# A packed row table read and written by indirect DMAs, weight rings of six slots split in place, and the next expert's rows turned after the last turn

## What is computed

```python
logits = xf @ w_router + b_router
top_logit, top_idx = lax.top_k(logits, 2)
top_w = softmax(top_logit)
# each position is a row of two experts; for the rows of expert e:
out = (silu(xb @ w1[e]) * (xb @ w3[e])) @ w2[e]
# y[position] = sum over its two experts of top_w * out
```

## Time and profile before

| | |
|---|---|
| median of 3 runs | 1771.09 us (1769.48 to 1774.81) |
| the profiled execution | 1762.26 us, its span 1760.5 us |
| mean granted clock of TensorE in it | 0.98 |
| TensorE busy (matmuls) | 1648.9 us, 94% |
| VectorE busy | 1357.8 us, 77% |
| ScalarE busy | 1022.7 us, 58% |
| GpSimd busy | 69.7 us, 4% |
| read from HBM, written to it | 518.85 MB, 15.47 MB |

### The profile page before, as it was taken

The page is one execution under the profiler, slowest core; times in us unless marked ns, Lnnn a source line. Parts: engine busy times, 40 slices in busy tenths (PEclk is TensorE's granted clock), DMA queues, the critical chain, the costliest instruction groups (busy, mean ns, idle before and its releaser), DMA issues.

```text
span 1760.5 us, 20788 instructions
## 1 busy us (share of the span) xinstructions
PE 1648.9 (94%) x7272; PEld 1275.6 (72%) x7273; DVE 1357.8 (77%) x1147; ACT 1022.7 (58%) x824; POOL 69.7 (4%) x85
## 2 busy tenths in 40 slices
PE   6999897999999998999999989999899999999995
PEld 2587756888587765777877768888677777787773
DVE  5687765775797776889888886565588888888888
ACT  1375432334266433778777775545577877777773
POOL 1200030000100001000000000000000000000200
PEclk9999998999999998999999999999999999999998
DMA  9885459874496445999999996666699999999992
GB/s 365 308 317 186 144 190 394 320 273 148 166 341 220 148 168 192 394 396 371 393 374 356 395 384 226 215 221 213 217 369 388 375 395 395 391 388 341 389 393 109
DMA packets 217236, 526.64 MB, mean 299 GB/s; under 512 B 9889, under 2 KB 14161, under 8 KB 217185
## 3 DMA queue, kind: packets, MB, share of 16 engines
q1 hardware_dynamic: 208770, 496.15, 77.1%
q0 software_dynamic: 8336, 29.55, 4.6%
q10 hardware_dynamic: 80, 0.26, 0.0%
HBM read 518.85 MB, written 15.47 MB: 304 GB/s over the span
## 4 chain that ended last, share of the span: by engine, by line
PE 78%; DVE 10%; issue 5%; DMA 3%; ACT 2%; ACTq 0%; DVEq 0%; SPq 0%
PE ps L1535 19%; PE ps L1537 19%; PE ps L1536 18%; PE ps L1541 5%; PE ps L1542 4%; DVE w_lo L1391 4%; PE ps L1546 4%; DMA w_raw<-in_ffn_w_dram 2%; PE ps L2036 2%; PE ps L2067 1%; DMA w_raw<-in_w_mod_mix_dram 1%; PE ps L1576 1%; ACT w_hi L814 1%; DVE gates L1170 1%; DMA w_raw<-in_w_in_dram 1%
## 5 line engine op out<-in xcount | busy, mean ns | idle before, releaser
L1391 DVE TENSOR_TENSOR w_lo<-w_raw,w_hi 128x2048 fp32r<-128x2048 f32 x333 | 756.5, 2288 | 173.4 <-ACT w_hi L814 171.1
L814 ACT CAST w_hi<-w_raw 128x2048 fp32r<-128x2048 f32 x333 | 633.6, 1910 | 178.9 <-PE ps L1542 86.9
L1535 PE MATMUL ps<-w_hi,actT_hi 128*128 128x512 f32 (+1 forms) x1464 | 583.2, 398 | 48.0 <-DVE w_lo L1391 17.3
L1537 PE MATMUL ps<-w_hi,actT_lo 128*128 128x512 f32 (+1 forms) x1464 | 569.0, 389 | 0.0
L1536 PE MATMUL ps<-w_lo,actT_hi 128*128 128x512 f32 (+1 forms) x1464 | 568.3, 388 | 0.0
L1535 PEld LDWEIGHTS ps<-w_hi,actT_hi 128*128 128x128 f32 x1464 | 278.1, 190 | 123.7 <-issue 35.0
L1537 PEld LDWEIGHTS ps<-w_hi,actT_lo 128*128 128x128 f32 x1464 | 277.8, 190 | 57.6
L1536 PEld LDWEIGHTS ps<-w_lo,actT_hi 128*128 128x128 f32 x1464 | 278.6, 190 | 53.9 <-issue 1.7
L954 DVE TENSOR_TENSOR w_lo<-w_raw,w_hi 128x2048 fp32r<-128x2048 f32 x81 | 185.4, 2289 | 104.0 <-ACT w_hi L551 103.7
L551 ACT CAST w_hi<-w_raw 128x2048 fp32r<-128x2048 f32 x81 | 154.5, 1908 | 132.4 <-PE ps L1537 91.9
L1541 PE MATMUL ps<-w_hi,gT_hi 128*128 128x512 f32 x448 | 182.3, 407 | 8.6 <-DVE gT_hi L1418 5.4
(11 more groups left out here) (281 smaller groups left out, 1204.7 us busy)
## 6 DMA issues: line engine op xcount, KB each, us to landing
w_raw<-in_exp_w_dram SPq DMA_DIRECT2D x336, 1024.0 KB, 7.6
w_raw<-in_ffn_w_dram SPq DMA_DIRECT2D x33, 1024.0 KB, 5.4
w_raw<-in_w_mod_mix_dram SPq DMA_DIRECT2D x24, 1024.0 KB, 11.4
w_raw<-in_w_mod_ffn_dram SPq DMA_DIRECT2D x24, 1024.0 KB, 5.7
w_raw<-in_w_gate_dram SPq DMA_DIRECT2D x24, 1024.0 KB, 6.7
w_raw<-in_w_in_dram SPq DMA_DIRECT2D x14, 1024.0 KB, 6.4
w_raw<-in_w_out_dram SPq DMA_DIRECT2D x8, 1024.0 KB, 5.1
by_row<-constants_dram POOLq DMA_DIRECT2D x16, 512.0 KB, 18.4
```

What stands on the lines that cost most here:

```text
L814: nc.scalar.copy(w_hi[:, i % SPLIT, :], w_raw[:, i % RING, :]).then_inc(split_hi, 1)
L1391: TTn(w_lo[:, i % SPLIT, :], w_raw[:, i % RING, :], w_hi[:, i % SPLIT, :].bitcast(F32), ALU.subtract).then_inc(piece_used, 1)
L1535: MM(to, hi, w_h, start=first, stop=False)
L1537: return MM(to, lo, w_h, start=False, stop=last)
```

## The change

- **Table.** `by_row` has 512 rows instead of 2048: expert e's rows begin where those of the experts before it end (`row_first`, a sum of counts). The clearing and its zeros are gone. `row_of` holds, for each expert and block, the table row of every place, and a number out of bounds for places at or beyond the count; loads and stores are indirect DMAs on GpSimd with a bounds check that skips those places. Both blocks' stores now go through GpSimd, ScalarE's `send_second` is gone.
- **Rings.** `w_hi` has six buffers (`SPLIT = 6`). `w_lo` lies on the same memory as `w_raw`, slot by slot, so VectorE splits in place. SyncE therefore reuses a slot when TensorE has used the piece (`split_used`; for a `mod` piece still `piece_used`). Memory use is the same. `LAG`, `LATE` and `UNSPLIT` keep the three steps that `SPLIT` stood for elsewhere. ScalarE and VectorE run one piece further ahead in the expert loop and split four pieces of the first expert before it.
- **Turns.** With one block `turn` writes bank 6 (`turned_bank`) and `turn_previous` stands behind A0 instead of inside B0, without its wait for the SiLU. `turn_rows` stands behind the last `turn`, in banks 2 and 3. Rows are handed over by halves of the width: the next expert's A0 waits for the first, A1 for the second.

```diff
-RING, SPLIT = 6, 3
+RING, SPLIT = 6, 6
+UNSPLIT = 3
+LAG = 3
+LATE = 3
...
+def turned_bank(blocks, b):
+    return HW1 + 2 if blocks == 1 else HW1 + 2 * b
...
-TURN_EARLY, TURN_LATE = (6, 7), (5, 7)
+NOWHERE = 1 << 20
+TURN_FREE, TURN_LATE = (2, 3), (5, 7)
...
+        w_hi = sb("w_hi", [P, SPLIT, PIECE], F32R)
+        in_place = ExitStack()
+        w_lo = sb("w_lo", [P, RING, PIECE], F32R, scope=in_place)
+        in_place.close()
         w_raw = sb("w_raw", [P, RING, PIECE])
-        w_hi = sb("w_hi", [P, SPLIT, PIECE], F32R)
-        w_lo = sb("w_lo", [P, SPLIT, PIECE], F32R)
...
-        by_row = nc.dram_tensor("by_row", (EXPERTS * SEQ, D), F32).ap()
+        by_row = nc.dram_tensor("by_row", (2 * SEQ, D), F32).ap()
...
                 for i, piece in enumerate(stretch.pieces):
-                    if i < RING:
-                        sp.wait_ge(piece_used, base + i + 1 + (gap if i < RING // 2 else 0))
-                    elif i < RING + stretch.raw:
-                        sp.wait_ge(split_used, split_base + i - RING + 1 + SPLIT)
+                    old = before.pieces[before.n - RING + i] if i < RING else stretch.pieces[i - RING]
+                    if old[0] == "mod":
+                        sp.wait_ge(piece_used, base + i + 1 - (0 if i < RING else stretch.raw))
+                    elif i < RING:
+                        sp.wait_ge(split_used, split_base + before.split_no[before.n - RING + i] - before.n_split + 1 + SPLIT)
                     else:
-                        sp.wait_ge(piece_used, base + i + 1 - stretch.raw)
+                        sp.wait_ge(split_used, split_base + stretch.split_no[i - RING] + 1 + SPLIT)
...
-                    for n in range(EXPERTS * TT):
-                        gp.dma_start(by_row[n * P:(n + 1) * P, :], consts[:, C_ZERO:C_ZERO + D]).then_inc(rows_cleared, 16)
...
                     def load_rows(e, b):
-                        gp.dma_start(xrows[:, b, :], by_row[e * SEQ + b * P:e * SEQ + (b + 1) * P, :]).then_inc(rows_loaded[b], 16)
+                        gp.indirect_dma_start(out=xrows[:, b, :], out_offset=None, in_=by_row[:, :], in_offset=rows_of(e, b),
+                                              bounds_check=2 * SEQ - 1, oob_is_err=False).then_inc(rows_loaded[b], 16)
+
+                    def send_sums(e, b):
+                        gp.indirect_dma_start(out=by_row[:, :], out_offset=rows_of(e, b), in_=hbuf[:, b, :], in_offset=None,
+                                              bounds_check=2 * SEQ - 1, oob_is_err=False).then_inc(y_sent_rows, 16)
...
                         gp.wait_ge(y_act, e + 1)
                         gp.wait_ge(y_dve, e + 1)
-                        gp.dma_start(by_row[(e - 1) * SEQ:(e - 1) * SEQ + P, :], hbuf[:, 0, :]).then_inc(y_sent_rows, 16)
-                        gp.wait_ge(y_sent_rows, e * 16)
+                        gp.wait_ge(rows_loaded[0], e * 16)
+                        gp.wait_ge(rows_loaded[1], e * 16 + 16)
+                        for b in range(2):
+                            send_sums(e - 1, b)
+                        gp.wait_ge(y_sent_rows, e * 32)
                         gp.sem_inc(y_home, 1)
...
-                                TTn(w_lo[:, i % SPLIT, :], w_raw[:, i % RING, :], w_hi[:, i % SPLIT, :].bitcast(F32),
+                                slot = EXPERT.slot(i)
+                                TTn(w_lo[:, slot, :], w_raw[:, slot, :], w_hi[:, i % SPLIT, :].bitcast(F32),
...
                             def panel(done, at, folds, last):
-                                rest_at(7, done)
+                                if blocks == 1:
+                                    gT_part(at)
+                                rest_at(8, done)
                                 if packed:
                                     fold_add(0, folds)
-                                rest_at(8, done)
-                                gT_part(at)
                                 rest_at(9, done)
+                                if blocks == 2:
+                                    gT_part(at)
+                                rest_at(10, done)
                                 gate_of(7, done, at, folds)
...
-                    step(STT(rest, number, float(SEQ), pos, ALU.mult, ALU.add))
+                    counted = ps[:, ROUTE + 1, 16:24]
+                    ahead_of = pick_w[:, 0, 0:EXPERTS * EXPERTS].rearrange("p (e f) -> p e f", f=EXPERTS)
+                    square = [P, EXPERTS, EXPERTS]
+                    step(TTn(ahead_of, iota[:, 0:EXPERTS].unsqueeze(1).broadcast_to(square), iota[:, 0:EXPERTS].unsqueeze(2).broadcast_to(square), ALU.is_lt))
+                    step(TTn(ahead_of, ahead_of, counted.unsqueeze(1).broadcast_to(square), ALU.mult))
+                    step(RED(row_first, ahead_of, AX_X, ALU.add))
+                    step(TTn(rest, pos, row_first.unsqueeze(1).broadcast_to(wide), ALU.add))
...
+                    step(RED(place_in[:, 0, :], tri, AX_X, ALU.add))
+                    step(TS(place_in[:, 1, :], place_in[:, 0, :], float(P), None, ALU.add))
+                    for b in range(2):
+                        TS(row_if[:, b, :], row_first, place_in[:, b, :], None, ALU.add)
+                    for b in range(2):
+                        ins = TS(pos[:, b, :], counted, place_in[:, b, :], float(-NOWHERE), ALU.is_ge, ALU.mult)
+                    step(ins)
+                    for b in range(2):
+                        ins = STT(row_of[:, b, :], row_if[:, b, :], float(NOWHERE - 1), pos[:, b, :], ALU.add, ALU.add)
+                    ins.then_inc(row_of_ready, 1)
...
                                 pe.wait_ge(silu_ready, at)
-                                up(4, "A", 0, done)
+                                up(4, "A", 0, done, turn_previous if blocks == 1 else None)
                                 up(5, "A", 1, done)
                                 pe.wait_ge(gated_ready, at)
-                                up(6, "B", 0, done, turn_previous)
+                                up(6, "B", 0, done, turn_previous if blocks == 2 else None)
...
-                            if blocks == 1:
-                                with pe.If(e < EXPERTS - 1):
-                                    turn_rows(0, e + 1, TURN_EARLY)
-                                turn(panel_0 + NP)
-                                with pe.If(e > EXPERTS - 2):
-                                    turn_places()
-                            else:
-                                turn(panel_0 + NP)
-                                with pe.If(e < EXPERTS - 1):
-                                    turn_rows(0, e + 1, TURN_LATE)
-                                with pe.Else():
-                                    turn_places()
+                            turn(panel_0 + NP)
+                            with pe.If(e < EXPERTS - 1):
+                                turn_rows(0, e + 1, TURN_FREE if blocks == 1 else TURN_LATE)
+                            with pe.Else():
+                                turn_places()
```

More of the change, by code:

```diff
@@ L953, in rest_of_piece @@
                 dve.wait_ge(split_hi, split_base + j + 1 - RAW_UP_TO.get(split_base, RAW_PIECES))
-                TTn(w_lo[:, j % SPLIT, :], w_raw[:, i % RING, :], w_hi[:, j % SPLIT, :].bitcast(F32),
+                slot = stretch.slot(i)
+                TTn(w_lo[:, slot, :], w_raw[:, slot, :], w_hi[:, (j - stretch.raw) % SPLIT, :].bitcast(F32),
                     ALU.subtract).then_inc(piece_used, 1)
```

273 lines of the change are left out of this document (140 added, 133 removed).

## The result

The changed kernel takes 1755.75 us in the median of 4 runs (1754.97 to 1756.87), the kernel before 1771.24 in the median of 4. The ratio is 0.9916 (95% interval 0.9896 to 0.9937), so 15.5 us less. The forecast was 38 us less. The time lies at the upper end of the range on record (1714 to 1757) and inside that of the rival "the ring brings nothing" (1750 to 1756).

The account below looks back on a forecast made before the run. TensorE was taken as the bound, with VectorE and DMA floors within 1.5 us per few panel. Experts -24 and clearing -14 sum to -38 us: 1724 from the profiled 1762.3, 1733 for the median; range 1714 to 1757.

Parts of the forecast that it names:

- the ring brings nothing: Rival, 17%: in-order queues let the DMA run dry, few panels stay at 16.2 or 16.3 us; total 1750 to 1756.
- The clearing: Dense layer: without the row table's clearing, TensorE gets back its waits and slow clock, 14 us.
- its gap might stay: Rival, 5%: with only raw pieces in hand the dense stage keeps some 8 of the 14 us; total 1741.
- The rings: Expert layer: with six w_hi buffers rounding stops waiting for the product three pieces back; 1.0 us idle per few panel goes.
- the DMA's floor of 16.0: Expert panels with up to 64 rows: they should go from 16.30 us to the DMA's floor, 16.0.
- Starvation: Rival, 5%: a slot's loop outlasts six pieces where landings average above 8.7 us; slower than before, 1778 us or more.
- Begin with a full ring, which lends some: Four few experts behind the router, a mid or the packed one: taken as 112 us, -4.5 each, -18.
- VectorE is through one split and it by then (3.0 us). Nothing.: Expert panels, turn_previous two pieces earlier: VectorE finishes gated before its product is due, so no cost.
- few after few: A few expert (up to 64 rows) following another: from 116.5 us to the DMA's 113.0, -3.5.
- The turns: Ends of single-block experts: last transposes before next rows, rows by halves; about 2.0 us per few expert, 1.1 per mid.
- The rows: Single-block experts: row transfers fall from 4.0 us of DMA to 1.3; issuing and VectorE's row numbers cost nothing.
- The base: Whole kernel: -38 us on the profiled 1762.3 gives 1724; the median's 8.8 us difference is kept, giving 1733.

Follow-up runs that it names:

- x7: The changed kernel with turns and ScalarE/VectorE order as before, keeping the new rings: 1762.3 us.
- x4: The changed kernel with the clearing's sixteen 512 KB copies put back, into a table that nothing reads: 1768.5 us.
- x10: The kernel before, unchanged, run again with a profile of its own: 1771.5 us in the median, the profiled execution 1775.1.
- x6: The changed kernel with rings and ScalarE/VectorE order as before, keeping the new turns: 1745.1 us.
- x2: The changed kernel with the rings of before (three w_hi, three separate w_lo), keeping new turns and order: 1802.4 us.
- x12: The changed kernel without the second pair of the four gathers started in the last expert (output not the reference's): 1755.6 us.
- x13: The changed kernel again, nothing altered, measured together with two of its part versions: 1756.3 us.
- x9: The changed kernel with only the ScalarE/VectorE order as before (one piece less ahead), new rings and turns kept: 1746.9 us.
- x5: The changed kernel with rings, turns and order all as before; no clearing, packed rows and handing over by halves stay: 1757.7 us.
- x8: The changed kernel with the experts' row transfers as plain DMAs of whole blocks instead of indirect ones (output not the reference's): 1763.1 us.
- x14: The changed kernel with only the order as before, new rings and turns kept, measured again in a later group: 1748.2 us.

## Why the prediction was wrong

Two steps failed. The gain inside the panels was put down to the ring, and x7 shows that the ring gives none of it. And the longer lead of ScalarE and VectorE had no term in the sum, and costs 8.1 us.

**The clearing** was right in mechanism and size: 14 forecast, 12.8 by x4. The 14.2 between the two first traces is one pair of executions; against x10's trace the same place comes 18.8 us earlier. That its gap might stay (a rival) did not happen.

**The rings: this step failed**, with "In a few panel that wait is what ends last ... with six it can. The 1.0 us of idle goes." The rounding did wait for the product, but removing that wait (x7) left 16.30 and 0.68. It was the last one on record, not what set the pace. ScalarE in x7, in a few panel:

```profile
733.15 0.60 ACT L850 ACTIVATE silu<-ps 128x512 f32<-128x512 f32 x1 [0.91 <-PE ps L1569]
733.64 1.91 ACT L840 CAST w_hi<-w_raw 128x2048 fp32r<-128x2048 f32 x1
736.18 0.38 ACT L864 ACTIVATE gT_hi<-ps 128x256 fp32r<-128x256 f32 x1 [0.63 <-PE ps L2071]
736.46 3.71 ACT L840 CAST w_hi<-w_raw 128x2048 fp32r<-128x2048 f32 x2
```

Both B pieces had landed (at 732.7 and 735.3), and their roundings stand behind a SiLU and a `gT_hi` that wait for TensorE. With those waits behind the product's, the loop closes in the same 16.3 us. That these two are what holds it is read from the list; what was shown is that the ring does nothing for it, and that the turns (x6) and the order (x2) bring 16.07 and 15.98. The end value, the DMA's floor of 16.0, was right by luck: turns and order brought it, not the ring.

**Starvation** was judged by a mean: a slot's loop closes with landings up to 8.7. The landings in the changed kernel's first expert, and in its last one:

```profile
DMA to landing us min/median/max: 6.1/8.0/9.4
```

```profile
DMA to landing us min/median/max: 6.0/8.4/11.6
```

In the median the loop closes. What was left out is the stock: by the 2.66 us of a piece, nine in hand hide an estimated 8 us more of a hold-up than six. x12 shows one place where six let it through, the burst of gathers (2.1 MB, 5.3 us) in the last expert: it takes 1.9 to 3.7 of the 3.9 to 4.6 us that the ring costs. That the rest goes at heads and branches is a reading of the traces, not shown. "Begin with a full ring, which lends some" was booked as a gain; it is lent from a smaller ring than before.

**The order one piece further ahead** was not priced at all; it is one sentence of front matter and no term of the sum. It brings 0.04 to 0.09 us in a few panel, 1 to 2 us in all, and costs at both ends of an expert: `gated` and the SiLU stand behind one more piece, which in those stretches hasn't landed. 8.1 us net. "VectorE is through one split and it by then (3.0 us). Nothing." failed here: with `gated` later, the first panels wait 4.17, 2.49 and 2.28 us. (The new order with the old turns wasn't tried.) What it did to the sum shows in the sixth expert, the "few after few" that was to go from 116.5 to 113.0 us. Its windows in the changed kernel, in x13 and in x9, which has the old order:

```profile
1370.79:1486.14 115.35, 111.04 (x486) 89.08 (x487) 99.44 (x59) 86.29 (x59) 5.38 (x4) 0.98 1.00 373
1363.74:1480.61 116.87, 110.52 (x487) 88.75 (x486) 104.14 (x61) 89.79 (x63) 8.31 (x4) 0.99 1.02 382
1367.57:1481.34 113.77, 109.48 (x487) 87.12 (x487) 103.15 (x61) 89.20 (x63) 6.24 (x4) 1.00 1.04 393
```

With the old order that term is nearly met.

**The turns** were forecast at 2.0 us per few expert and 1.1 per mid one, 12.2 in all with the halves, though the sum let the DMA's floor take most of it. The last panel of the first expert went from 23.66 us to 23.11 by the halves (x5) and to 21.96 by the turns (x6). All in all the turns gave 12.6, of which about 4.6 are the twenty few panels that each got 0.23 shorter, which had been put down to the ring.

**The rows** were priced at 2.7 us of DMA per expert, and the 7.8 MB less are 2.5 us each at 394 GB/s. x8 says that plain whole blocks would cost 7 us in the changed kernel, and x5 that packed rows and halves against those of before came to nothing (1757.7 against 1771.2 - 12.8 = 1758.4). What x5's trace shows against it is the entry into the loop: VectorE's first split comes 12.2 us after TensorE's first product there, 7.5 before, and TensorE stands 4.41 us for it. The first expert was to take 4.5 us less; from the second router product to its end it takes 142.5 us, and took 140.7. The forecast's "Nothing" looked at VectorE's added operations and not at that entry. Whether these operations, their place in the code or something else in the change lengthens it is open.

So: clearing 12.8 + turns 12.6 - ring 3.9 - order 8.1 = 13.4, measured 15.5. The 2.1 between them are less than the medians of before differ by. (The kernel before without its clearing was not tried: unused rows would be unset.)

**The base.** The sum was made against a profiled execution of 1762.3 and moved up by 8.8 to the median. x10 shows part of what the 8.8 are: that execution was without the long branch, which is in 13 of 17 profiles, and it also lost less at the clearing. The changed kernel's own executions differ in the same way (its second profile is 5.8 us shorter than its first), so moving the whole sum by one pair's difference is a guess. Two traces compared (7.4 us) would have hidden half of the gain.

The line on a DMA's time that the prediction takes from the Trainium skill (DMA: Bandwidth & Descriptors, Anatomy of one DMA) is given there for DMAs issued from GpSimd, and the pieces come from SyncE. The forecast did not rest on it.

## What to carry to other kernels

A wait that ends last is only the first of several that may close at the same time: before a buffer is added for it, ask what stands next in the same list. Buffers in flight are a stock, and a stretch whose DMA is the bound lives on it at every irregularity, so count what a shared or in-place ring takes away there, not only whether its loop closes in the mean. And when an engine's in-order list is moved one step ahead, look at the first and the last turn of the loop: work that was in time inside it stands behind data that hasn't come.

## What the runs showed of the hardware

TensorE's branch at the start of the sixth expert took 5.2 to 6.8 us in 13 of 17 profiles and was short in the other four. The two profiles of before differ in it, and so do the two of the changed kernel and the two of ring and turns (x9, x14): it is the execution, not the program. In all 13 the instruction queue moved three packets (0.05 MB) between 1320 and 1430 us, in the four none, so it is code that was fetched; what decides whether it must be is open. It lengthens that panel by 4.6 to 5.7 us between two profiles of one kernel. With the next panel taken in it is 6.9 us in the kernel before and 2.8 in the changed one, where the short branch uncovers the wait for `gated`.

Two branches around the packed expert (3.2 to 6.6 us) and one behind the router (3.9 to 7.5) were there in every profile. That one was 3.9 to 4.3 us in all kernels with `w_lo` in place and 7.0 to 7.5 in those with the old rings. VectorE's entry into the expert loop took 0.5 us in both profiles of before and 2.8 to 6.2 in all others. These kernels differ in their code in more than one way, so that the layout of the code sets such prices is likely and not shown.
